# Banded attention with high and low query halves stacked in the partitions, values as the stationary operand, and results stored turned

## The chip, the cores and the metric

The kernel runs on one core of one Trainium2 chip. The metric is the device time of the core in microseconds (us), the median of three runs: 2661.86 us for the kernel before (2660.55 to 2664.36).

## The reference, cut to what matters

The whole program is a hybrid encoder block over 2048 tokens of width 1024: one projection of x, two attention mixers, a merge, a layer norm, a mixture of experts and a second layer norm. The change touches mixer A and the places where its result is read.

```python
proj = h @ w_in[l]
aq, ak, av, bq, bk, bv, gpre = jnp.split(proj, IN_SPLITS, axis=-1)
aq = apply_rope(aq ...)      # 8 heads of 64
ak = apply_rope(ak ...)      # 2 heads of 64
oa = swa_sink_attention(aq, ak, av, sinks[l])

def swa_sink_attention(q, k, v, sinks):      # chunks of 64; own chunk and the previous one
    sc = einsum('bnqkgd,bnjkd->bnkgqj', qc, kb) * (d ** -0.5)
    m = maximum(max(sc, -1), sink)
    e = exp(sc - m)
    p = e / (sum(e, -1) + exp(sink - m))
    o = einsum('bnkgqj,bnjkd->bnqkgd', p, vb)

mix = (ga * (oa @ w_proj_a[l]) + gb * (ob @ w_proj_b[l])) @ w_out[l]
```

## The kernel before, in words

Every number is float32, and products on TensorE are made from two parts of a number, a high part (the value rounded to the engine's fast format) and a low part (what is left), as high x high + low x high + high x low. ScalarE makes the high part with a copy, VectorE the low part with a subtraction. A PSUM tensor is turned (transposed) by TensorE with an identity.

The program has phases, each with its own semaphores and a barrier at its end. The phase with the prefix `j` is the projection of q, k and v with the banded attention A inside it; `b` is attention B with the gate projection; `m` the merge; then routing and the experts. Names of tensors carry the prefix: `j_qa` is `qa` of phase j.

**Projection phase (L144 to L895).** It goes over 16 tiles of 128 tokens. `over_tiles` writes tiles 0, 1, 14 and 15 out and the others as a loop of two tiles a turn. Each engine has its own program, and its order is written by hand. On TensorE a middle tile t is: `group` 0 (24 products of 512 columns: the A queries), `scores_of(t-1, g)` for the two key heads g, group 1 (24 products of 256 columns: A keys and values), `turn_p(t-1, 0)`, group 2, `turn(t, 0)`, `turn_p(t-1, 1)`, `values_of(t-1, 0)`, group 3, `turn(t, 1)`, `turn(t, 2)`, `values_of(t-1, 1)`, group 4, `turn(t, 3)`. So the attention of a tile runs inside the next tile's projection.

- `scores_of(t, g)` makes four blocks of 128 queries x 128 keys into one PSUM bank. The stationary operand is `qa[rows, half]`: 64 partitions of key head g, high or low in the free dimension. A block is three products, L427 (high q, high k), L428 (high q, low k), L429 (low q, high k).
- VectorE takes maxima (`maxima`, L742 to L747). ScalarE makes the exponentials with their sums (`exps`, L556). VectorE makes the denominators and their reciprocals (`invert`, L752, L754). TensorE turns the four blocks of exponentials (`turn_p`, L440). ScalarE and VectorE split them into `th` and `tl` (L565, L758).
- `values_of(t, g)` has the turned exponentials stationary and 128 columns of values (high and low of one head side by side) moving: L451 and L452, eight products for each g.
- `result` (L765, L767, L770, VectorE) adds the halves and multiplies by the reciprocals. `store_o` (SyncE) writes the result to `oa`, tokens x 512, in four DMAs a tile, with 256 bytes in a run.
- GpSimd has one add for each rotation (`add`, L519). `rotate` is VectorE's part of it (L794, L797, L799). `pieces` and `low` split the turned q and k into high and low (L584, L811).
- After the last tile SyncE stores its result (L274), and the phase's barrier follows. `load_chunk0` has by then loaded what attention B starts with, the four lambda vectors among it (L294).

**Merge phase (L1491 to L2007).** It also goes over 16 tiles. Tile t's 512 columns of `oa` and 512 of `ob` are loaded to `oin`. TensorE turns all 8 pieces of 128 columns (`turn`, L1671) into `pt`. ScalarE and VectorE split them (`high_ab` L1815, `low_ab` L1929), and the products with w_proj_a, w_proj_b and w_out follow. Tile t+1 is turned before the w_out product of tile t-1. GpSimd adds the gated halves (L1894).

Of the kernel before, what the change touches and what calls it, by code (L numbers as in the profile page):

```python
# [95 lines left out]
O_STORES = 16 * 4  # L96


class Chunk0:


    def __init__(self, ph, lam):
# [8 lines left out]
        self.lam = lam  # L111
# [32 lines left out]
def project_phase(nc, x_cols, w_in, positions, inv_freq, sinks, w_hi, w_lo, cos_t, sin_t, nsin_t, ident, xt_hi, xt_lo, qk_hi, qk_lo, v_hi, v_lo, oa,  # L144
# [15 lines left out]
    with Phase(nc, "j") as ph:  # L160
        x_in = chunk0.rows[:, 0, :]
        pr = chunk0.rows[:, 1, 0:BANK].rearrange("p (b n) -> p b n", b=NB)
        o = chunk0.rows[:, 1, BANK:].rearrange("p (c g j d) -> p c g j d", c=2, g=A_KV, j=2)
# [3 lines left out]
        by_sin = ph.sb("by_sin", [P, BANK])  # L167
# [6 lines left out]
        qa = ph.sb("qa", [P, 2, A_Q], F32R)  # L174

        ks = ph.sb("ks", [P, 2, 3 * CHUNK], F32R)
# [29 lines left out]
        pv, o_halved, o_added, o_scaled, o_stored = ph.sem("pv"), ph.sem("o_halved"), ph.sem("o_added"), ph.sem("o_scaled"), ph.sem("o_stored")  # L206
        block = ph.block()
        ROT = [j for j, g in enumerate(GROUPS) if g[1]]
        PG = [0, 1, 2, 0, 1]
        STAGED0 = {2: 0, 3: B_QK // P}  # L210
# [30 lines left out]

        def staged_of(half, r):
            if r == 0:
                return qa[:, half, :].rearrange("p (c i n) -> p c i n", c=2, n=CHUNK)
            if r == 1:
                return ks[:, half, 0:P]
            return (qkh, qkl)[half][:, STAGED0[r]:STAGED0[r] + GROUPS[ROT[r]][1] // P, :].rearrange("p i n -> p (i n)")

# [12 lines left out]
        def _(sp):  # L261
# [22 lines left out]
            def load_chunk0():  # L284
# [8 lines left out]
                for n, lam in enumerate(lambdas):  # L293
                    sp.dma_start(chunk0.lam[:, n, :], lam.to_broadcast([P, HD])).then_inc(chunk0.lam_in, 16)  # L294
# [43 lines left out]
            store_rows(sp, STAGED0[2], STAGED0[3], slice(SEQ - P, SEQ), last_stored)  # L338
            sp.wait_ge(v_lo_done, 2 * (NT - 1) + 4)
# [19 lines left out]
        def _(pe):  # L359
            pe.sem_inc(transposed, 2)  # L360

            def group(t, u, j):
# [4 lines left out]
                if j == 0:  # L367
# [8 lines left out]
                for k in range(KD):  # L376
# [12 lines left out]
                last.then_inc(product[j], 1)  # L389
# [17 lines left out]
            def scores_of(t, g, last_tile):  # L407
                pe.wait_ge(qk_lo_done, 4 * t + 4)
                if last_tile:
                    if g:  # L410
                        pe.wait_ge(scaled, 4 * t + 7)
                else:
                    after(pe, o_added, 2 * t + g - 1)
                rows = slice(g * HD, (g + 1) * HD)
                qh, ql = (qa[rows, half, :] for half in range(2))
                for b in range(NB):
                    out = blocks(unit_bank(g, last_tile))[:, b, :]
                    if b >= 2:
                        k_hi, k_lo = (ks[rows, half, 0:P] for half in range(2))
                    elif isinstance(t, int) and t == 0:  # L420
                        k_hi, k_lo = (ks[rows, half, 0:CHUNK] for half in range(2))
                        out = out[:, 0:CHUNK]
                    else:
                        k_hi, k_lo = (ks[rows, half, :].rearrange("p (n c) -> p n c", c=CHUNK)[:, 0:3:2, :] for half in range(2))
                        out = out.rearrange("p (n c) -> p n c", c=CHUNK)
# [17 lines left out]
            def values_of(t, g, u, last_tile):  # L443
# [3 lines left out]
                for b in range(NB):  # L447
# [2245 lines left out]
```

## Time and profile before

| | |
|---|---|
| median of the runs | 2661.86 us |
| the profiled execution's own time | 2663.14 us |
| its span, first to last instruction | 2661.4 us |
| TensorE busy (matmul / weight load) | 94% / 79% |
| VectorE, ScalarE, GpSimd busy | 62%, 46%, 17% |
| mean granted TensorE clock | 0.969 |
| DMA | 535.86 MB, 201 GB/s |

Busy shares are of the whole span; the phases have different limits, so what an edit is worth has to be read in its phase. The projection phase lies at about 15 to 548 us of the span, attention B at 550 to 1243 us, the merge at 1244 to 1676 us. PE is the TensorE matmul, PEld its weight load, DVE VectorE, ACT ScalarE, POOL GpSimd, SP SyncE. A matmul's duration in the trace is its latency; how fast matmuls follow one another is read from the distance of their starts.

### The profile page before, as it was taken

What the parts mean: (1) busy time and instruction counts of PE and PEld (TensorE: products, weight loads), DVE (VectorE), ACT (ScalarE), POOL (GpSimd) and SP (SyncE); (2) the same over time, 40 slices, a digit from 0 to 9 for tenths busy, and PEclk for the clock granted to TensorE, in tenths of its full rate; (3) what the DMA queues carried; (4) which work ended last, traced back from release to release, by engine and by line L of the source; (5) the groups of instructions that cost most, each with busy time, mean ns of one, the idle gap of its engine ahead of it and who ended that gap; (6) DMA issues with size and microseconds to landing.
All of it is one profiled execution on the core that took longest, in us unless ns stands there. A gap on an engine that the chain in (4) does not pass through costs nothing. (4 is left out here: it accounts for less than half of the span.)

```text
span 2661.4 us, 42306 instructions
## 1 busy us (share of the span) xinstructions
PE 2491.0 (94%) x12879; PEld 2092.6 (79%) x12880; DVE 1658.8 (62%) x3322; ACT 1217.2 (46%) x2075; POOL 452.3 (17%) x526
## 2 busy tenths in 40 slices
PE   5999999979999999998999999499999999999990
PEld 4888888868888888887788887388888888888880
DVE  5655455567677776766644455775785557657856
ACT  4333232244454544545111112375785557657856
POOL 0111111110110111100223331111211121112110
PEclk9999999989999999999999999599999999999995
DMA  6333333566756757535544434487897789769957
GB/s 199 122 106 102 102 102 102 153 182 194 213 182 194 216 172 205 196 132 214 177 136 139 142 111 166 171 293 278 284 382 245 226 296 327 242 225 324 381 158 260
DMA packets 233100, 535.86 MB, mean 201 GB/s; under 512 B 42945, under 2 KB 93377, under 8 KB 230961
## 3 DMA queue, kind: packets, MB, share of 16 engines
q1 hardware_dynamic: 164560, 422.55, 45.9%
q0 software_dynamic: 16416, 56.57, 8.8%
q10 hardware_dynamic: 52032, 55.61, 6.0%
q8 instruction: 48, 0.79, 0.1%
q14 instruction: 44, 0.35, 0.0%
HBM read 415.63 MB, written 119.01 MB: 201 GB/s over the span
## 5 line engine op out<-in xcount | busy, mean ns | idle before, releaser
L2543 DVE TENSOR_TENSOR e_wl<-rw_raw,e_wh 128x1024 fp32r<-128x1024 f32 (+1 forms) x384 | 446.6, 1218 | 24.7 <-ACT e_wh L2456 24.6
L2456 ACT ACTIVATE e_wh<-rw_raw 128x1024 fp32r<-128x1024 f32 (+1 forms) x384 | 376.9, 1049 | 6.5 <-PEq L74 6.5
L1228 PE MATMUL b_pg<-b_g_wh,jb_w_low 128*128 128x512 f32 x1024 | 336.6, 402 | 1.4 <-DVE b_g_out L1437 1.1
L2406 PE MATMUL e_p_gu<-e_wh,e_xh 128*128 128x512 f32 (+1 forms) x784 | 310.8, 396 | 0.8 <-DVE e_xl L2548 0.8
L2408 PE MATMUL e_p_gu<-e_wl,e_xh 128*128 128x512 f32 (+1 forms) x784 | 306.4, 391 | 0.0
L2407 PE MATMUL e_p_gu<-e_wh,e_xl 128*128 128x512 f32 (+1 forms) x784 | 305.9, 390 | 0.0
L1228 PEld LDWEIGHTS b_pg<-b_g_wh,jb_w_low 128*128 128x128 f32 x1024 | 185.1, 189 | 36.1 <-issue 3.8
L1286 ACT ACTIVATE b_th<-b_t 128x512 fp32r<-128x512 f32 (+3 forms) x160 | 85.3, 533 | 263.4 <-PE b_t L1210 255.2
L1228 PE MATMUL b_pg<-b_g_wl,jb_w_low 128*128 128x512 f32 x512 | 204.5, 400 | 0.0
L1377 DVE TENSOR_SCALAR_CACHE_REDUCE b_sc<-b_s 128x512 f32<-128x512 f32 (+4 forms) x320 | 175.8, 580 | 34.8 <-PE b_s L1199 32.7
L386 PE MATMUL j_pg<-qkv_w_hi,j_xh 128*128 128x512 f32 (+1 forms) x512 | 192.4, 376 | 2.4 <-DVE qkv_w_lo L682 2.4
L388 PE MATMUL j_pg<-qkv_w_lo,j_xh 128*128 128x512 f32 (+1 forms) x512 | 187.6, 366 | 0.0
L387 PE MATMUL j_pg<-qkv_w_hi,j_xl 128*128 128x512 f32 (+1 forms) x512 | 187.0, 365 | 0.0
L2408 PEld LDWEIGHTS e_p_gu<-e_wl,e_xh 128*128 128x128 f32 x784 | 147.6, 188 | 31.4
L2406 PEld LDWEIGHTS e_p_gu<-e_wh,e_xh 128*128 128x128 f32 x784 | 147.7, 188 | 30.9 <-issue 1.2
L2407 PEld LDWEIGHTS e_p_gu<-e_wh,e_xl 128*128 128x128 f32 x784 | 147.9, 189 | 28.3
L2418 PE MATMUL e_py<-e_wh,e_hh 128*128 128x512 f32 x392 | 161.1, 411 | 0.0
L1279 ACT ACTIVATE b_sc<-b_sc,b_nb 128x128 f32<-128x128 f32 (+15 forms) x128 | 153.1, 1196 | 17.5 <-DVE b_nb L1392 17.5
L519 POOL TENSOR_TENSOR j_by_cos<-j_by_cos,j_by_sin 128x512 f32<-128x512 f32 x64 | 82.9, 1296 | 448.4 <-DVE j_by_sin L799 448.4
L2420 PE MATMUL e_py<-e_wl,e_hh 128*128 128x512 f32 x392 | 154.2, 393 | 0.0
L1422 DVE TENSOR_TENSOR b_tl<-b_t,b_th 128x512 fp32r<-128x512 f32 (+3 forms) x160 | 97.5, 610 | 90.3 <-ACT b_th L1286 89.1
L2419 PE MATMUL e_py<-e_wh,e_hl 128*128 128x512 f32 x392 | 153.8, 392 | 0.0
(414 smaller groups left out, 5529.3 us busy)
## 6 DMA issues: line engine op xcount, KB each, us to landing
rw_raw<-w_gate_up SPq DMA_DIRECT2D x256, 512.0 KB, 6.3
rw_raw<-w_down SPq DMA_DIRECT2D x128, 512.0 KB
jb_w_low<-xt_hi SPq DMA_DIRECT2D x64, 512.0 KB, 3.8
jb_w_low<-xt_lo SPq DMA_DIRECT2D x64, 512.0 KB, 4.8
gates<-b_g_out ACTq DMA_DIRECT2D x64, 256.0 KB, 5.8
m_gt<-gates SPq DMA_DIRECT2D x16, 1024.0 KB, 8.3
jb_lead<-qk_hi SPq DMA_DIRECT2D x36, 256.0 KB, 7.1
jb_lead<-qk_lo SPq DMA_DIRECT2D x36, 256.0 KB, 7.8
```

The costliest lines, as they stand in the source:

```text
L386: nc.tensor.matmul(out, xh[:, u, at], wh, start=(k == 0), stop=False)
L387: nc.tensor.matmul(out, xl[:, u, at], wh, start=False, stop=False)
L388: last = nc.tensor.matmul(out, xh[:, u, at], wl, start=False, stop=(k == KD - 1))
L1228: last = nc.tensor.matmul(pg[:], x_side, w_side, start=(q == 0), stop=(q == PASSES - 1))
L1377: last = nc.vector.tensor_scalar(sc[u][:, m, ks.start:end], bank[n % 4][:, 0:end - ks.start], 1.0, NEG, ALU.mult, ALU.max, accum_out=mx[:, ...
L2406: nc.tensor.matmul(p_gu[p][:], xh[:, at], hi, start=(k == 0), stop=False)
L2407: nc.tensor.matmul(p_gu[p][:], xl[:, at], hi, start=False, stop=False)
L2408: last = nc.tensor.matmul(p_gu[p][:], xh[:, at], lo, start=False, stop=(k == KD - 1))
L2418: nc.tensor.matmul(py[:, js], hh[:, at], wh[:, n, js], start=(k == 0), stop=False)
L2420: last = nc.tensor.matmul(py[:, js], hh[:, at], wl[:, n, js], start=False, stop=(k == KF - 1))
L2456: nc.scalar.activation(wh[:, slot(e, s), :], raw[:, s:s + 1, :], ACT.Copy).then_inc(w_hi, 1)
L2543: nc.vector.tensor_tensor(wl[:, slot(e, s), :], raw[:, s:s + 1, :], f(wh[:, slot(e, s), :]), ALU.subtract).then_inc(w_lo, 1)
```

## The change

The score products take a stacked stationary operand. `qa` and `ks` get the key head g in the free dimension, and in the partitions the high part of q in the 64 rows of head g and the low part in the other 64; `ks` has the high part of k in both halves, and the low part of k is in a tensor `kl` of its own. A block then is two products: `qa[:, g]` (128 partitions) with `ks[:, g]`, which makes high x high and low x high at once, and `qa[rows, g]` (64 partitions) with `kl[rows]`. So splitting q and k takes one instruction for each head and half, and a copy for k.

The exponentials are multiplied by the reciprocal before they are turned (`normalise` in place of `invert`). The values are stationary and the turned exponentials move: three products of 256 columns for each of the two chunks, and the output is the result already turned, head dimension in the partitions. `result` becomes one copy of 64 partitions. `oa` is stored turned (8 heads x 64 x tokens), with two DMAs a tile and 512 bytes in a run, and the merge loads it turned: it turns only the `ob` pieces, and splits the `oa` half straight from SBUF (`high_a`, `low_a`). On TensorE `turn_p` stands now in the middle of groups 2 and 3, and `by_sin` lies in the space of `lg`, so the lambda vectors are loaded after the last rotation.

```diff
@@ projection phase
-        qa = ph.sb("qa", [P, 2, A_Q], F32R)
-        ks = ph.sb("ks", [P, 2, 3 * CHUNK], F32R)
+        qa = ph.sb("qa", [P, A_KV, A_Q], F32R)
+        ks = ph.sb("ks", [P, A_KV, 3 * CHUNK], F32R)
+        kl = ph.sb("kl", [P, 3 * CHUNK], F32R)
...
             def store_o(t, done=o_stored):
-                sp.wait_ge(o_scaled, 2 * t + 2)
-                for c in range(2):
-                    for s in range(2):
-                        sp.dma_start(oa[bass.ds(t * P + c * CHUNK, CHUNK), :].rearrange("q (b s d) -> q b s d", s=2, d=HD)[:, :, s, :],
-                                     o[s * CHUNK:(s + 1) * CHUNK, c].rearrange("p g j d -> p (g j) d")).then_inc(done, 16)
+                sp.wait_ge(o_made, 2 * t + 2)
+                for g in range(A_KV):
+                    sp.dma_start(oa[g * GH:(g + 1) * GH, :, bass.ds(t * P, P)].rearrange("h d n -> d h n"),
+                                 o[g * HD:(g + 1) * HD].rearrange("p h c n -> p h (c n)")).then_inc(done, 16)
...
-                    nc.tensor.matmul(out, qh[:, bs], k_hi, start=True, stop=False)
-                    nc.tensor.matmul(out, qh[:, bs], k_lo, start=False, stop=False)
-                    last = nc.tensor.matmul(out, ql[:, bs], k_hi, start=False, stop=True)
+                    nc.tensor.matmul(out, qa[:, g, bs], k_hi, start=True, stop=False)
+                    last = nc.tensor.matmul(out, qa[rows, g, bs], k_lo, start=False, stop=True)
...
             def turn_p(t, g, own_tile):
-                pe.wait_ge(exped, m + 1)
+                pe.wait_ge(p_scaled, m + 1)
...
-                for b in range(NB):
-                    v = (own[:, u] if b >= 2 else back[:])[:, :, g * HD:(g + 1) * HD]
-                    nc.tensor.matmul(out, th[:, bs], v, start=True, stop=False)
-                    last = nc.tensor.matmul(out, tl[:, bs], v, start=False, stop=True)
+                for c in range(2):
+                    v = own[:, u] if c else back[:]
+                    cs = slice(c * 2 * P, (c + 1) * 2 * P)
+                    nc.tensor.matmul(out, v[:, 0, :], th[:, cs], start=True, stop=False)
+                    nc.tensor.matmul(out, v[:, 0, :], tl[:, cs], start=False, stop=False)
+                    last = nc.tensor.matmul(out, v[:, 1, :], th[:, cs], start=False, stop=True)
...
-            def invert(t, g):
+            def normalise(t, g):
                 nc.vector.reciprocal(inv[:, g, :], den[:, g, :]).then_inc(summed, 1)
+                dve.wait_ge(summed, 2 * m + 2)
+                nc.vector.tensor_tensor(pr, pr, inv[:, g, :].unsqueeze(2).to_broadcast([P, NB, P]), ALU.mult).then_inc(p_scaled, 1)
...
+                    if r < 2:
+                        for g in range(A_KV):
+                            own_rows, others = rows_of(g), rows_of(1 - g)
+                            if r == 0:
+                                low_part = banded_of(r, g, others)
+                            else:
+                                nc.vector.tensor_copy(banded_of(r, g, others), f(banded_of(r, g, own_rows)))
+                                low_part = kl[own_rows, 0:P]
+                            done = nc.vector.tensor_tensor(low_part, turned_of(r, last)[own_rows], f(banded_of(r, g, own_rows)), ALU.subtract)
@@ merge phase
-                    turn(oin[:, 1 - u, :], ab_turned)
+                    turn(oin[:, 1 - u, :], ab_turned, range(KA, KD))
...
+            def high_a(t, k, u):
+                act.wait_ge(oin_in[u], 32 * (k + 1))
+                if not (isinstance(t, int) and t == 0):
+                    act.wait_ge(a_done, t)
+                nc.scalar.activation(abh[:, 0:A_Q], oin[:, u, 0:A_Q], ACT.Copy).then_inc(a_hi, 1)
...
+            def low_a(t, u):
+                dve.wait_ge(a_hi, t + 1)
+                nc.vector.tensor_tensor(abl[:, 0:A_Q], oin[:, u, 0:A_Q], f(abh[:, 0:A_Q]), ALU.subtract).then_inc(a_lo, 1)
```

What the change does to the order of two engines in the looped tile of the projection phase is shown at two places. First TensorE, at the start of `scores_of` right behind group 0; `j_pa0` is the PSUM bank of the first key head. Before:

```order
L428 MATMUL j_pa0<-j_ks,j_qa 128x128
L429 MATMUL j_pa0<-j_ks,j_qa 128x128
L427 MATMUL j_pa1<-j_ks,j_qa 128x128
L428 MATMUL j_pa1<-j_ks,j_qa 128x128
L429 MATMUL j_pa1<-j_ks,j_qa 128x128
```

These are the end of the last block of head 0 and the first block of head 1, three products a block. In the changed kernel the same place reads:

```order
L399 MATMUL j_pg0<-jb_w0,j_xl 128x512
L400 MATMUL j_pg0<-jb_w0_low,j_xh 128x512
L421 ISA
L220 ISA
L444 MATMUL j_pa0<-j_ks,j_qa 128x128
L445 MATMUL j_pa0<-j_kl,j_qa 128x128
L444 MATMUL j_pa0<-j_ks,j_qa 128x128
```

L444 has 128 partitions, L445 has 64, and they take turns through all eight blocks. Then VectorE, from the rotation of group 2 (three rows) to the split of the second head's exponentials. Before:

```order
L794 TENSOR_TENSOR j_by_cos<-j_pg,qkv_cos 128x512
L797 TENSOR_TENSOR j_by_sin<-j_pg,qkv_nsin 128x8x32
L799 TENSOR_TENSOR j_by_sin<-j_pg,qkv_sin 128x8x32
L811 TENSOR_TENSOR j_qa<-j_pt,j_qa 128x512
L752 TENSOR_TENSOR j_den<-j_sums,j_se 128x4
L753 ISA
L754 RECIPROCAL j_inv<-j_den 128x4
L758 TENSOR_TENSOR j_tl<-j_pt,j_th 128x512
```

And in the changed kernel, where L785 is the new multiplication and L844 the low part of q:

```order
L819 TENSOR_TENSOR j_by_cos<-j_pg,qkv_cos 128x512
L822 TENSOR_TENSOR lg<-j_pg,qkv_nsin 128x8x32
L824 TENSOR_TENSOR lg<-j_pg,qkv_sin 128x8x32
L781 TENSOR_TENSOR j_den<-j_sums,j_se 128x4
L782 ISA
L783 RECIPROCAL j_inv<-j_den 128x4
L784 REGISTER_ALU
L785 TENSOR_TENSOR jb_rows<-jb_rows,j_inv 128x512
L844 TENSOR_TENSOR j_qa<-j_pt,j_qa 64x512 x2
L796 COPY jb_rows<-j_pa 64x512
L789 TENSOR_TENSOR j_tl<-j_pt,j_th 128x512
```

The denominators now stand right behind the rotation, with a multiplication of 128x512 behind them on which TensorE's second `turn_p` waits.

## Rows read from the trace of the kernel before

**Rows 1.** Busy us by stretch; columns PE, PEld, DVE, ACT, POOL, clock, DMA share, GB/s.

```profile
200.00:500.00 300.00, 300.00 (x1718) 257.95 (x1717) 154.15 (x356) 93.42 (x293) 50.34 (x39) 1.00 0.33 102
1270.00:1600.00 330.00, 329.67 (x1567) 274.91 (x1566) 161.16 (x211) 37.19 (x56) 95.30 (x40) 1.00 0.41 139
```

**Rows 2.** Timeline of PE around one tile's scores; start us, duration us, then the instruction.

```profile
225.62 0.39 PE L388 MATMUL j_pg<-jb_w_low,j_xh 128*128 128x512 f32 x1
225.94 0.32 PE L427 MATMUL j_pa<-j_ks,j_qa 64*128 64x128 f32 x1
...
228.17 0.27 PE L429 MATMUL j_pa<-j_ks,j_qa 64*128 64x128 f32 x1
228.38 0.39 PE L386 MATMUL j_pg<-qkv_w_hi,j_xh 128*128 128x256 f32 x1
228.60 0.28 PE L387 MATMUL j_pg<-qkv_w_hi,j_xl 128*128 128x256 f32 x1
228.72 0.29 PE L388 MATMUL j_pg<-qkv_w_lo,j_xh 128*128 128x256 f32 x1
```

**Rows 3.** Timeline of PEld (weight loads) at the end of those scores.

```profile
228.00 0.19 PEld L428 LDWEIGHTS j_pa<-j_ks,j_qa 64*128 64x128 f32 x1
228.11 0.19 PEld L429 LDWEIGHTS j_pa<-j_ks,j_qa 64*128 64x128 f32 x1
228.37 0.19 PEld L386 LDWEIGHTS j_pg<-qkv_w_hi,j_xh 128*128 128x128 f32 x1
```

**Rows 4.** Timeline of PE: before, in and behind `values_of` for one head.

```profile
237.03 0.39 PE L388 MATMUL j_pg<-qkv_w_lo,j_xh 128*128 128x512 f32 x1
237.27 0.60 PE L404 MATMUL j_pt<-ident,j_by_cos 128*128 128x128 f32 x4
237.70 0.60 PE L440 MATMUL j_pt<-ident,jb_rows 128*128 128x128 f32 x4
238.06 0.30 PE L451 MATMUL j_pa<-j_back,j_th 128*128 128x128 f32 x1
...
238.98 0.45 PE L386 MATMUL j_pg<-qkv_w_hi,j_xh 128*128 128x512 f32 x1
```

**Rows 5.** Timeline of DVE in the same tile.

```profile
238.91 0.41 DVE L799 TENSOR_TENSOR j_by_sin<-j_pg,qkv_sin 128x256 f32<-128x256 f32 x1
239.24 0.68 DVE L811 TENSOR_TENSOR j_qa<-j_pt,j_qa 128x512 fp32r<-128x512 f32 x1
239.84 0.89 DVE L752 TENSOR_TENSOR j_den<-j_sums,j_se 128x4 f32<-128x4 f32 x1
```

**Rows 6.** Timeline of POOL in the same tile; the number before the idle time is its duration.

```profile
239.40 1.30 POOL L519 TENSOR_TENSOR j_by_cos<-j_by_cos,j_by_sin 128x512 f32<-128x512 f32 x1 [6.29 <-DVE j_by_sin L799]
```

**Rows 7.** Timeline of DVE in the merge: a multiplication of 128x512 in SBUF.

```profile
1250.43 0.69 DVE L1923 TENSOR_TENSOR jb_rows<-jb_rows,m_ri 128x512 f32<-128x512 f32 x1
```

**Rows 8.** Timelines, first tile and last tile, PE.

```profile
53.38 0.45 PE L404 MATMUL j_pt<-ident,j_by_cos 128*128 128x128 f32 x1 [8.05 <-DVE j_qa L811]
...
517.26 0.30 PE L404 MATMUL j_pt<-ident,j_by_cos 128*128 128x128 f32 x1 [1.07 <-DVE j_qa L811]
```

**Rows 9.** Timelines of the phase's end, DVE, then SP's queue.

```profile
545.00 0.42 DVE L765 COPY jb_rows<-j_pg 128x256 f32<-128x256 f32 x1 [0.32 <-PE j_pg L452]
...
545.91 0.42 DVE L770 TENSOR_TENSOR jb_rows<-jb_rows,j_inv 128x256 f32<-128x256 f32 x1
...
546.37 2.51 SPq L274 DMA_DIRECT2D oa<-jb_rows  x4
550.27 0.64 SPq L1044 DMA_DIRECT2D jb_lead<-qk_hi  x1
```

**Rows 10.** Merge: all turns of `oin`; count, least/median/greatest ns, first and last start, form.

```profile
L1671 PE MATMUL m_pt<-ident,jb_rows x128: 270/272/476, 1244.3 to 1588.3; 128*128 128x128 f32 x128
```

**Rows 11.** Merge: the longest wait of PE; us in total, times, longest.

```profile
PE m_psa L1680 <- DVE m_abl L1929: 3.2, 1, 3.2
```

**Rows 12.** Timeline of POOL in the merge's second step.

```profile
1264.41 2.36 POOL L1894 TENSOR_TENSOR m_pa<-m_pa,m_pb 128x1024 f32<-128x1024 f32 x1 [19.06 <-DVE m_pb L1981]
```

More of the change, by code:

```diff
@@ L209, in project_phase @@
         PG = [0, 1, 2, 0, 1]
+        HALVES = range(0, KD // 2), range(KD // 2, KD)
         STAGED0 = {2: 0, 3: B_QK // P}
@@ L338, in _ @@
             store_rows(sp, STAGED0[2], STAGED0[3], slice(SEQ - P, SEQ), last_stored)
+            sp.wait_ge(rotated, 4 * NT + 2)
+            for n, lam in enumerate(lambdas):
+                sp.dma_start(chunk0.lam[:, n, :], lam.to_broadcast([P, HD])).then_inc(chunk0.lam_in, 16)
             sp.wait_ge(v_lo_done, 2 * (NT - 1) + 4)
@@ L360, in _, with group @@
             pe.sem_inc(transposed, 2)
-            def group(t, u, j):
+            def group(t, u, j, ks_=range(KD)):
                 first = isinstance(t, int) and t == 0
                 c0, rot, v = GROUPS[j]
-                if j == 0:
+                if ks_[0]:
+                    pass
+                elif j == 0:
                     pe.wait_ge(scaled, 4 * t + 4)
@@ L375, in group @@
                     pe.wait_ge(v_lo_done, 2 * t + 3)
-                for k in range(KD):
+                for k in ks_:
                     if first and k % QK == 0:
@@ L388, in group @@
                     last = nc.tensor.matmul(out, xh[:, u, at], wl, start=False, stop=(k == KD - 1))
-                last.then_inc(product[j], 1)
+                if ks_[-1] == KD - 1:
+                    last.then_inc(product[j], 1)
             def turn(t, r, last_tile):
@@ L488, in tile @@
                     turn(t, 0, last)
+                    group(t, u, 2, HALVES[0])
+                    turn(t, 1, last)
                     turn_p(t - 1, 0, False)
[L490 to L491 removed]
+                    group(t, u, 2, HALVES[1])
                     scores_of(t, 0, True)
+                    values_of(t - 1, 0, 1 - u, False)
+                    group(t, u, 3, HALVES[0])
                     turn_p(t - 1, 1, False)
[L494 to L496 removed]
+                    group(t, u, 3, HALVES[1])
                     scores_of(t, 1, True)
                     turn(t, 2, last)
+                    values_of(t - 1, 1, 1 - u, False)
                     turn_p(t, 0, True)
@@ L850, in tile @@
                         over_tables(1, 9, 13)
-                    result(t - 1, 0, False)
                     if second:
@@ L1668, in _, with turn @@
         def _(pe):
-            def turn(src, done, ks=range(KD)):
+            def turn(src, done, ks):
                 for k in ks:
@@ L1739, in step @@
                 first = isinstance(t, int) and t == 0
-                if first:
-                    pe.wait_ge(first_lo, 1)
-                elif is_tile(t):
-                    pe.wait_ge(ab_lo, t + 1)
+                if is_tile(t):
+                    pe.wait_ge(a_lo, t + 1)
+                    if not first:
+                        pe.wait_ge(ab_lo, t + 1)
                 second = isinstance(t, int) and t == 1
@@ L1747, in step @@
                     pe.wait_ge(mixed, t)
-                    turn(pa, m_turned)
+                    turn(pa, m_turned, range(KD))
                 if is_tile(t):
@@ L1762, in step @@
                         pe.wait_ge(mixed, t)
-                        turn(pa, m_turned)
+                        turn(pa, m_turned, range(KD))
                     if is_tile(t - 1):
@@ L1785, in step @@
                     product(psw, mh, ml, range(KD), KA + KB, w_done, isinstance(t, int) and t == 1)
-            pe.wait_ge(oin_in[0], 32)
-            turn(oin[:, 0, :], first_turned, range(0, KA))
             over_steps(pe, step)
```

141 lines of the change are left out of this document (72 added, 69 removed).

## The prediction

> **What bounds the kernel now.** I read the stretches first (busy time by window), because both phases that the change touches have to be judged by their own limit. From 200 to 500 us, looped tiles of the projection phase, TensorE is busy 300.00 of 300.00 us at full clock, VectorE 154, ScalarE 93, GpSimd 50; from 1270 to 1600 us, the merge, TensorE is busy 329.67 of 330 us [rows 1]. The list of waits has nothing for TensorE in the looped tiles. So in both stretches the time is the sum of TensorE's slots, and everything else counts only if it makes TensorE wait. A slot is not the duration in a row (that is latency) but the distance of two starts. Then I read the timeline of matmuls and of weight loads in one tile, VectorE and GpSimd beside them, and last the two ends of the phase, where TensorE does wait.
>
> **Scores: fewer products, but each in another array mode than the one before.** In the steady stream of 64-row products one weight load follows another after 0.11 us (228.00, 228.11) [rows 3]. The 24 products of a tile with their surroundings go from 225.62 (last product of group 0) to 228.60 (second product of group 1), 2.98 us; less a slot of 0.23 for 512 columns and one of 0.12 for 256 (228.60 to 228.72) they cost 2.63 us [rows 2]. In these are two changes of the number of rows, marked 128*128 and 64*128. At the second, the next weight load comes 0.26 us after the last one, not 0.11 (228.11, 228.37) [rows 3]: it is not loaded beside the running product, but behind it. At the first, 0.32 us lie between starts where a 512-column product takes 0.23 [rows 2]. It is the same in all 14 middle tiles.
>
> The changed kernel has 16 products in place of 24, but a 128-row and a 64-row product alternate, as the order shows. The first follows group 0 in its own mode; behind each of the 16 the mode changes, the last time into group 1. At 0.26 us each that is 4.16 us a tile, against 2.63: **+1.53 us a tile, +24.5 us over 16 tiles.** The trace has no alternation, so this is bounded: from above by 0.26; the start-to-start distance of the matmuls themselves at a change is 0.21 (228.17 to 228.38) [rows 2], and if that were all, 16 x 0.21 = 3.36 us, +0.73 a tile, +11.7. If a change cost nothing once it happens on every product, 16 x 0.11 = 1.76 us, -0.87 a tile, -13.9. I take 0.26, because it is the distance of two loads, and every load stands behind a change here.
>
> The Trainium skill has rules for both ends. "TensorEngine Tiling (Array Packing)", Key Properties, says that going to another tiling mode empties the engine; by that rule, the sum is the forecast's, and the rows agree at the two changes a tile that they have. "TensorE: Matmul & The Clock Gate", LDWEIGHTS, prices a weight load by its columns and says that the number of rows doesn't matter; by that alone 64 and 128 rows could be mixed freely, and the sum would be that of the first rival.
>
> **Values.** Before, eight products take 0.92 us for a head (238.06 to 238.98) [rows 4], 1.84 a tile. Now there are twelve of 256 columns at 0.12 [rows 2]: 1.44. -0.40 a tile, -6.4 us. No mode changes here.
>
> **The new wait: `turn_p` for the second head behind the multiplication.** Group 2 ends at 237.03 + 0.23 = 237.26. TensorE then has `turn(t, 0)` (0.43, four turns, 237.27 to 237.70 [rows 4], so 0.109 each), the values (0.72) and half of group 3 (12 x 0.227 = 2.72), and would turn the exponentials at 241.13. On VectorE the rotation's last operation starts at 238.91 and lets the next start at 239.24 [rows 5]; now the denominators stand there, the reciprocal, and a multiplication of 128x512, 0.69 us [rows 7]. But GpSimd's add for this rotation runs from 239.40 to 240.70 [rows 6], and beside it a VectorE operation on SBUF alone doesn't get through: the 128x4 addition of the denominators took 0.89 us and ended at 240.73 [rows 5], while the subtraction before it, which reads PSUM, took its usual 0.68. So the multiplication starts to work at 240.70 and ends at 241.39: TensorE waits about 0.3 us a tile, 14 tiles, **+4 us**. From 0 (if it gets in before GpSimd) to 0.6 a tile (if the denominators are held too), 8 us. Behind the waiting `turn_p` stand the rest of group 3 and all that follows; the low part of p then is ready at about 243.7, and `turn(t, 2)`, which waits for it, comes at 244.3, so it costs once.
> The skill's page "SBUF — State Buffer", in SBUF: two separate sides, calls the pair of ports that VectorE and GpSimd share an exclusive lock, taken also by a VectorE operation with two SBUF inputs against a GpSimd operation that reads SBUF. By it the loser waits for the whole add, as the 0.89 us show; if ports were shared by bandwidth, the term would be near 0.
>
> The first head's multiplication stands behind the maxima, with 1.5 groups of products (some 5.6 us) as cover, and its denominators are ready some 1.5 us after the exponentials: hidden. The other edits of the tile are VectorE and ScalarE time beside a full TensorE: two subtractions of q for one (+0.68), two copies and one more subtraction for k (about +0.7), two multiplications (+1.4), one copy in place of three operations of 0.42 in `result` (-0.6 for each head). VectorE goes from 154/300 to about 57%; nothing there is late by the rows, and if one were, the price is again a wait at a turn. `store_o` has two DMAs for four, off the path within the loop.
>
> **Ends of the projection phase.** In the first tile TensorE waits 8.05 us for the low part of q, and one more copy (0.6) and one more subtraction (0.68 [rows 5]) stand in that chain: +1.3. In the last tile a wait of 1.07 us for the same [rows 8] goes, as half of group 2 now stands before `turn(t, 1)`: -1.1. At the end, the last result took VectorE from 545.00 to 546.33 and SyncE four issues in 2.51 us, and the next phase begins 1.4 us later [rows 9]. One copy of 0.7 in place of the three (-0.6) and two issues (-1.25): -1.9. The four lambda loads move past SyncE's last stores of q and k; SyncE has the gap between those and the last values' store for it, and the lambdas are used only some 6 us into the next phase: 0, and up to +2 if the last values' store is pushed past the barrier.
>
> **Merge.** 128 turns of `oin` become 64 [rows 10]. For tiles 2 to 15 that is 14 x 4 x 0.109 = -6.1 us of TensorE's stream. For tile 0 the start hangs on ScalarE, no gain. For tile 1 TensorE already waits 3.2 us for the low part [rows 11], so its turns don't count, and the low part of the `oa` half now is a subtraction in SBUF, just when GpSimd adds for 2.36 us from 1264.41 [rows 12]: it is held to 1266.77, then 0.7, then the `ob` half 0.6: 1268.0, against 1266.4 before: +1.6. In later tiles the same hold lies under the w_out product, 48 slots of 0.227, 10.9 us. Runs of 512 bytes in place of 2 KB in the loads of `oa`: a load has a whole step for itself (96 slots and 16 turns, 23.5 us); 0.
>
> **The sum**, on the profiled execution's own 2663.14 us (2661.4 of span and 1.7 around it; 1.3 above the median): +24.5 - 6.4 + 4 + 1.3 - 1.1 - 1.9 - 6.1 + 1.6 = +15.9, 2679.0; against the median, 2677.8. I say 2677.5.
>
> **Rivals.**
> First, changes of mode cost nothing when they come on every product: the next weights are loaded beside the running product after all. -13.9 in place of +24.5: 2677.8 - 38.4 = 2639. For it: fewer products, no more columns, and the trace never shows two changes in a row. Against it: all 14 middle tiles show the 0.26 and the 0.32. It wins from a price per product below about 0.20 us: at 0.20 the 16 cost 3.20, +9.1 over the tiles, which the gains elsewhere just cancel. That is the case on the other side, 16%.
> Second, only the starts' distance of 0.21 counts: 2677.8 - 12.8 = 2665. 12%, about a third of it inside the bound of no change, the rest slower.
> Third, VectorE's extra work is later than I have it (the multiplication behind the denominators that are held as well, the k copies under GpSimd's last add, and then `turn(t, 3)`): 0.9 us a tile in place of 0.3, 14 tiles, +8.4: 2686. For it: three operations on SBUF alone are new in each tile, and GpSimd's add of 1.30 us lies right over one. Against it: VectorE is busy only 154 of 300 us [rows 1]. 8%.
> That the change doesn't do what it says is no case: the order shows 16 and 12 products where there were 24 and 16.
>
> **Numbers.** Forecast 64%, first rival 16%, second 12%, third 8%. The likeliest case alone spans 2670 to 2685. To leave out no more than two in ten, the range takes the second and most of the third and leaves out the first: 2655 to 2686. About 0.2% (5.3 us) is what a measurement can tell from no change: faster 18% (the first rival and a little beside), within it 12%, slower 70%.
>
> **What the profile after would show.** The scores of a middle tile last 4.2 us from group 0 to group 1, weight loads 0.26 apart and none pulled ahead; 3.4 or 1.8 us would be the rivals. The values last 0.72 for a head. A wait of about 0.3 us at the second `turn_p` of each tile, released by the multiplication, which is drawn out to 1.5 us or more. 1.9 us less between the last values and the next phase. Merge steps shorter by 0.44 us. I am wrong if the looped tiles get shorter.

## The result and the profile after

The changed kernel takes **2703.51 us** (median of 4 runs, 2701.86 to 2704.45) against 2662.43 us for the kernel before in the same session (2660.55 to 2664.36): ratio 1.0156, 95% interval 1.0143 to 1.0169. Slower, as forecast, but by 41 us and not by 16: 2703.5 lies outside the range of 2655 to 2686.

Where the 40.5 us between the two spans (2661.4 and 2701.9) are, by first and last start of TensorE in each phase: the projection phase, which went from 19.5 to 544.5 us, now goes from 19.3 to 588.6, **+44.2**; the gap behind it -0.9; attention B +0.8; the merge with the gap before it -4.4; the rest, experts above all, +0.8. So the merge did what was forecast, and the projection phase lost twice as much as it should have.

The stretches of the kernel after, us busy and count for PE, PEld, DVE, ACT, POOL, then the granted clock, the DMA share and GB/s. The first row answers to [rows 1]; the next three are each one looped tile, from its first score product to that of the next; the last three cut the tile that begins at 275.05.

```profile
200.00:500.00 300.00, 300.00 (x1471) 250.55 (x1470) 163.15 (x338) 93.05 (x292) 44.45 (x35) 0.94 0.31 101
242.22:275.05 32.83, 32.83 (x170) 27.17 (x169) 19.16 (x39) 11.50 (x34) 5.22 (x4) 1.00 0.32 103
275.05:310.80 35.75, 35.75 (x171) 29.88 (x169) 19.16 (x39) 10.21 (x33) 5.22 (x4) 0.90 0.29 96
379.45:413.77 34.32, 34.32 (x171) 28.66 (x169) 19.16 (x39) 11.50 (x34) 5.21 (x4) 0.95 0.30 99
275.05:278.15 3.10, 3.10 (x14) 2.17 (x12) 2.37 (x5) 0.00 (x0) 1.17 (x1) 1.00 0.79 270
278.15:284.98 6.83, 6.83 (x29) 6.36 (x30) 2.24 (x8) 1.60 (x9) 0.10 (x1) 0.50 0.00 0
284.98:290.00 5.02, 5.02 (x26) 4.11 (x25) 1.44 (x5) 1.98 (x9) 0.46 (x1) 1.00 0.00 0
```

TensorE still never waits (300.00 of 300.00), but the clock column reads 0.94 where it read 1.00. The tile that keeps its full clock takes 32.83 us; all tiles of before took 31.53. The others take 34.32 or 35.75: in them the granted clock is at its half level (1.2 of 2.4 GHz) once, for 3.4 or 6.8 us. It falls 3.1 to 4.9 us after the first score product, that is towards the end of the 16 or up to 0.9 us behind them (at 278.15, with the scores from 275.05 to 279.52), and it is mostly the dense products of group 1 that then run at half speed. So a fall of 3.4 us costs 34.32 - 32.83 = 1.49 us, one of 6.8 costs 2.92. Of the 13 tiles from 105 to 551 us two have no fall, nine the short one, two the long one: 446.13 us in all, 19.2 more than 13 full-clock tiles. The instructions are the same in all 13, so they alone don't decide where in a tile the clock falls, or whether it does.

The scores, timeline of PE, answering to [rows 2]: group 0 ends, then products of 128 and 64 rows in turn.

```profile
241.99 0.39 PE L400 MATMUL j_pg<-jb_w_low,j_xh 128*128 128x512 f32 x1
242.22 0.22 PE L444 MATMUL j_pa<-j_ks,j_qa 128*128 128x128 f32 x1
242.37 0.33 PE L445 MATMUL j_pa<-j_kl,j_qa 64*128 64x128 f32 x1
242.62 0.33 PE L444 MATMUL j_pa<-j_ks,j_qa 128*128 128x128 f32 x1
242.88 0.32 PE L445 MATMUL j_pa<-j_kl,j_qa 64*128 64x128 f32 x1
```

The starts are 0.25 to 0.26 us apart, the price that [rows 3] gave for one change of mode; 16 take 3.98 us where the 24 took 2.44.

The second `turn_p` and what it waits for, answering to [rows 4 to 6]: the timelines of DVE, of POOL and of PE.

```profile
257.09 0.15 DVE L781 TENSOR_TENSOR j_den<-j_sums,j_se 128x4 f32<-128x4 f32 x1
257.27 0.18 DVE L783 RECIPROCAL j_inv<-j_den 128x4 f32<-128x4 f32 x1
257.48 1.60 DVE L785 TENSOR_TENSOR jb_rows<-jb_rows,j_inv 128x512 f32<-128x512 f32 x1
```

```profile
257.25 1.29 POOL L541 TENSOR_TENSOR j_by_cos<-j_by_cos,lg 128x512 f32<-128x512 f32 x1 [6.32 <-DVE lg L824]
```

```profile
258.54 0.39 PE L399 MATMUL j_pg<-qkv_w_hi,j_xl 128*128 128x512 f32 x1
258.77 0.39 PE L400 MATMUL j_pg<-qkv_w_lo,j_xh 128*128 128x512 f32 x1
259.14 0.66 PE L456 MATMUL j_pt<-ident,jb_rows 128*128 128x128 f32 x4
```

The multiplication is drawn out to 1.60 us beside GpSimd's add, as forecast. It ends at 259.08, and TensorE turns 0.06 us later, at 259.14. The product before starts at 258.77, and its slot is 0.23 us (258.54 to 258.77), so TensorE could have turned at 259.00: it waits 0.14 us. Because the duration of a product reaches beyond its slot, the wait doesn't show as idle time of PE. In the list of waits it stands with the weight loads:

```profile
PEld j_pt L456 <- DVE jb_rows L785: 6.8, 14, 1.6
```

In each of the 13 tiles the `turn_p` starts 0.06 us behind the multiplication, and the slot in front of it is 0.36 to 0.40 us. The sum of the denominators (257.09) got in before the add (257.25), and the reciprocal took its 0.18 us beside it, where before the sum was held (0.89). TensorE came when I had it (3.89 us behind the end of group 2, forecast 3.87), and the add ended when I had it; but the multiplication ended 0.54 us behind the add (258.54) and not 0.69.

The waits of TensorE in the phase (us in total, times, longest), answering to [rows 8]:

```profile
PE j_pt L417 <- DVE j_qa L844: 9.1, 1, 9.1
...
PE j_pt L456 <- DVE jb_rows L785: 1.4, 2, 1.2
PE j_pt L417 <- DVE j_kl L844: 1.3, 1, 1.3
```

The first is the one of 8.05 us. The one of 1.2 (in the second line) is new and stands in tile 1 alone, where VectorE also makes the later tiles' sine tables.

The end of the phase in the timeline of SP's queue, answering to [rows 9]:

```profile
589.63 1.26 SPq L282 DMA_DIRECT2D oa<-jb_rows  x2
...
593.41 0.62 SPq L1081 DMA_DIRECT2D jb_lead<-qk_hi  x1
```

The merge's turns of `oin` (count, least/median/greatest ns, first and last start), answering to [rows 10]:

```profile
L1711 PE MATMUL m_pt<-ident,jb_rows x64: 270/273/330, 1297.3 to 1627.9; 128*128 128x128 f32 x64
```

The merge's second step, DVE and then POOL, answering to [rows 12]:

```profile
1309.04 2.57 DVE L1970 TENSOR_TENSOR m_abl<-jb_rows,jb_lead 128x512 fp32r<-128x512 f32 x1 [0.41 <-ACT jb_lead L1854]
1311.53 0.68 DVE L1974 TENSOR_TENSOR m_abl<-m_pt,jb_lead 128x512 fp32r<-128x512 f32 x1
```

```profile
1308.71 2.35 POOL L1936 TENSOR_TENSOR m_pa<-m_pa,m_pb 128x1024 f32<-128x1024 f32 x1 [19.39 <-DVE m_pb L2026]
```

64 turns for 128, and in the second step the low part, 2.57 us for 0.69, is held by the add until 1311.06, then takes the rest of its time: both as forecast. A later step takes 23.13 us for 23.58, and the one with the held low part is 1.5 us longer (20.37 for 18.85; forecast +1.6).

### The profile page after: what moved, and what is told of

The parts are those of the page before. It is cut to its first block and busy times, and to the rows that moved or that the text cites. A ratio compares the mean times of both kernels' runs of the same rounds, so it can differ in the third digit from the quotient of the medians.

```text
span 2701.9 us, 41856 instructions
## 1 busy us (share of the span) xinstructions
PE 2526.7 (94%) x12623; PEld 2109.1 (78%) x12624; DVE 1709.7 (63%) x3369; ACT 1236.4 (46%) x2137; POOL 457.4 (17%) x526
## 5 line engine op out<-in xcount | busy, mean ns | idle before, releaser
L398 PE MATMUL j_pg<-qkv_w_hi,j_xh 128*128 128x512 f32 (+1 forms) x512 | 203.2, 397 | 1.8 <-DVE qkv_w_lo L711 1.8
L399 PE MATMUL j_pg<-qkv_w_hi,j_xl 128*128 128x512 f32 (+1 forms) x512 | 197.1, 385 | 0.0
L400 PE MATMUL j_pg<-qkv_w_lo,j_xh 128*128 128x512 f32 (+1 forms) x512 | 196.7, 384 | 0.0
L2453 PEld LDWEIGHTS e_p_gu<-e_wl,e_xh 128*128 128x128 f32 x784 | 147.9, 189 | 31.6
L541 POOL TENSOR_TENSOR j_by_cos<-j_by_cos,lg 128x512 f32<-128x512 f32 x64 | 82.5, 1289 | 492.8 <-DVE lg L824 492.8
```

The source lines that it names most:

```text
L398: nc.tensor.matmul(out, xh[:, u, at], wh, start=(k == 0), stop=False)
L399: nc.tensor.matmul(out, xl[:, u, at], wh, start=False, stop=False)
L400: last = nc.tensor.matmul(out, xh[:, u, at], wl, start=False, stop=(k == KD - 1))
L2453: last = nc.tensor.matmul(p_gu[p][:], xh[:, at], lo, start=False, stop=(k == KD - 1))
```

## The experiments

A product's mode is here the number of rows, 64 or 128, that it uses. Theory A was: the alternation of modes costs its slots, and it also brings the clock down. Its rivals: the fall has another cause (B), or the slot isn't a matter of modes (C). In the cuts of code "..." stands for lines left out.

**e1: the same 16 products, four changes of mode.** The heads write different banks, so they can be interleaved; every second block begins with the low keys.

```diff
-                    scores_of(t - 1, 0, False)
-                    scores_of(t - 1, 1, False)
+                for b in range(NB):
+                    for n in range(4):
+                        g, low = n % 2, (n // 2 + b) % 2
...
+                        q, k = (qa[rows, g, bs], k_lo) if low else (qa[:, g, bs], k_hi)
+                        last = nc.tensor.matmul(out, q, k, start=n < 2, stop=n >= 2)
```

> The changed kernel with its 16 score products of a looped tile in another order: the two heads, which write different banks, side by side, and every second block with the low keys' products first, so that the row mode changes 4 times a tile and not 16 times. The products are the same. Theory A (the forecast's missing term: the alternation of 128-row and 64-row products costs its slots, and it also makes the granted clock fall to half for 3.4 us or more in nearly every tile, some 1.5 us a tile): scores 12 x 0.11 + 4 x 0.26 = 2.4 us in place of 4.0, that is -24 us over 15 tiles, and no half clock between 60 and 580 us, some -22 us more: about 2657 us. Theory B (the half clock has nothing to do with the alternation, it comes from the waits or from VectorE's new work): only -24, about 2679 us, half clock as before. Theory C (a change of mode costs nothing like 0.26, the slot grew for another reason, such as 64 rows read from the wide layout): no change, 2703 us.

Measured: 2650.43 us, ratio 0.9956 (0.9940 to 0.9973); full clock from 60 to 538 us, tiles of 30.70. A, and 7 us better than A. PE shows why:

```profile
255.62 0.33 PE L468 MATMUL j_pa<-j_ks,j_qa 128*128 128x128 f32 x2
255.88 0.44 PE L468 MATMUL j_pa<-j_kl,j_qa 64*128 64x128 f32 x4
256.25 0.66 PE L468 MATMUL j_pa<-j_ks,j_qa 128*128 128x128 f32 x4
256.84 0.44 PE L468 MATMUL j_pa<-j_kl,j_qa 64*128 64x128 f32 x4
```

Four products of 128 rows take 0.59 us to the next change, four of 64 rows 0.37. The 64 rows of one head lie in partitions 0 to 63, those of the other in 64 to 127: two such products run side by side (tested in f3 and f5). That tiles of one mode work in parallel stands in the Trainium skill, "TensorEngine Tiling (Array Packing)", Key Properties; the trace agrees, 0.37 against 0.59.

**e2: all 16 products with 128 rows.** The low keys get 128 rows for each head, the other head's are zero (cleared once by GpSimd).

```diff
-        kl = ph.sb("kl", [P, 3 * CHUNK], F32R)
+        kl = ph.sb("kl", [P, A_KV, 3 * CHUNK], F32R)
...
-                    last = nc.tensor.matmul(out, qa[rows, g, bs], k_lo, start=False, stop=True)
+                    last = nc.tensor.matmul(out, qa[:, g, bs], k_lo, start=False, stop=True)
```

> The changed kernel with the low keys in a tile of 128 rows for each head, the other head's rows zero, so that all 16 score products of a tile have 128 rows and the mode never changes. Theory A: 16 x 0.11 = 1.8 us a tile in place of 4.0 (-2.2 x 16 = -35), no half clock (-22): about 2646 us. Theory B: -35 alone, half clock stays: about 2668 us. Theory C (the slot isn't a matter of modes): 2703 us.

Measured: 2646.07 us, ratio 0.9941 (0.9925 to 0.9958). Scores 1.73 us a tile (products 0.11 apart), tile 30.59, full clock. As theory A has it; B and C fall, and the price of a change is (32.83 - 30.59) / 16 = 0.14 us on top of 0.11.

**e3: the scores' part undone**, with its layout, copies and subtractions; all else as changed.

```diff
...
-                    nc.tensor.matmul(out, qa[:, g, bs], k_hi, start=True, stop=False)
-                    last = nc.tensor.matmul(out, qa[rows, g, bs], k_lo, start=False, stop=True)
+                    nc.tensor.matmul(out, qh[:, bs], k_hi, start=True, stop=False)
+                    nc.tensor.matmul(out, qh[:, bs], k_lo, start=False, stop=False)
+                    last = nc.tensor.matmul(out, ql[:, bs], k_hi, start=False, stop=True)
```

> The changed kernel with one part undone: the scores as they were (three products of 64 rows a block, q and k in high and low halves of the free dimension, one copy and one subtraction for each). Values, the multiplication of p, the order of half groups and the merge stay changed. Theory A: the slots go back to 2.44 us a tile (-1.54 x 16 = -25) and the clock stays full (-22): about 2657 us, some 6 us under the kernel before. Theory B: half clock stays: about 2679 us. A third (the +44 us of the phase come largely from VectorE's new multiplication and the waits behind it): over 2690 us.

Measured: 2656.22 us, ratio 0.9979 (0.9969 to 0.9988), looped tiles of 31.39 at full clock. So the rest of the change is a small gain (0.14 us a tile, 1.1 in the last tile, 2.0 at the phase's end, the merge), and all of the loss lies in the scores: 47 us, of which 1.44 us a tile are slots.

One fall is left, in tile 1, and it is of use below. There the scores are those of tile 0, the first with only half of the keys: 12 of the 24 products of 64 rows have 64 moving columns in place of 128. They go from 66.06 to 68.50 us, and 0.8 us behind them the clock is at half:

```profile
66.06:69.31 3.25, 3.25 (x31) 3.18 (x31) 2.81 (x8) 1.61 (x3) 1.27 (x1) 1.00 0.93 309
69.31:72.72 3.41, 3.41 (x18) 3.41 (x17) 3.14 (x10) 1.28 (x9) 0.00 (x0) 0.50 0.01 2
```

The kernel before has the same 24 products there, and no fall.

**e4: the alternation in two stretches** with 12 dense products between them.

```diff
                     group(t, u, 0)
                     scores_of(t - 1, 0, False)
+                    group(t, u, 1, HALVES[0])
                     scores_of(t - 1, 1, False)
-                    group(t, u, 1)
+                    group(t, u, 1, HALVES[1])
```

> The changed kernel with the first half of group 1 (12 dense products, 2.7 us) put between the two heads' scores. As many products, as many changes of mode (16 a tile), but the alternation comes in two stretches of 2.0 us. Theory A1 (the clock falls because of one long alternation of 4.0 us): no half clock, about 2703 - 22 = 2681 us. Theory A2 (each short alternation is enough, or its share in the tile counts): half clock as before, about 2703 us. Theory B (no link with the alternation): 2703 us.

Measured: 2680.79 us, ratio 1.0073 (1.0056 to 1.0090). The looped tiles are 32.84 us and the clock is 1.00:

```profile
200.00:500.00 300.00, 300.00 (x1547) 248.16 (x1545) 175.11 (x357) 98.26 (x308) 48.45 (x37) 1.00 0.33 105
```

A1: nothing is taken away, the slots stay, and 22.7 us come back. This is the price of the clock, measured by itself. (The 12 products have 256 columns and take 1.54 us, not the 2.7 of the expectation.)

**f6: only 3 dense products between.**

Against e4:

```diff
-                    group(t, u, 1, HALVES[0])
+                    group(t, u, 1, range(0, 1))
                     scores_of(t - 1, 1, False)
-                    group(t, u, 1, HALVES[1])
+                    group(t, u, 1, range(1, KD))
```

> The changed kernel with only 3 dense products (0.4 us at 256 columns) of group 1 between the two heads' scores, where the earlier split had 12. If such a short break is enough: full clock, about 2681 us. If the two alternations count as one: half clock in nearly every tile, about 2703 us.

Measured: 2705.08 us, ratio 1.0166 (1.0145 to 1.0186), clock 0.95 from 200 to 500 us. 0.46 us of dense work doesn't help, 1.54 us does.

**f2: the new scores alone, in the kernel before.** The diff is that of e3 read backwards, on the other kernel; it also has `by_sin` in the space of `lg` and the lambda loads behind the last rotation, as the changed kernel has.

> The kernel before with the scores' part of the change alone (the layout of q and k, 16 products in two modes, and the copies and subtractions that belong to it); values, results and merge as before. If the slots and the clock together come from the alternation: 2662.4 + 1.54 x 16 (25) + 22 = about 2709 us, half clock in nearly every tile, and steady tiles without it of 31.53 + 1.54 = 33.07 us. If the clock needs the new order of values and turns beside it: 2687 us.

Measured: 2713.92 us, ratio 1.0203 (1.0186 to 1.0220), clock 0.94 from 200 to 500 us, tiles of 34.4 to 34.5 with the short fall and 35.9 with the long one. The fall needs nothing of the rest of the change but that move. It is 5 us above the expectation; 3 of them are that here not one tile keeps its full clock, where the changed kernel has two.

**f1: no alternation at all, but a long run.** The kernel before, each block's three 64-row products issued twice.

```diff
+                    for _ in range(2):
                         nc.tensor.matmul(out, qh[:, bs], k_hi, start=True, stop=False)
                         nc.tensor.matmul(out, qh[:, bs], k_lo, start=False, stop=False)
                         last = nc.tensor.matmul(out, ql[:, bs], k_hi, start=False, stop=True)
```

> The kernel before with the three 64-row products of every score block issued twice (48 a tile in place of 24): a run of short products in one mode, about 5.1 us long, longer than the alternation of 4.0 us. If the clock falls because TensorE computes with short or half-high products for so long: half clock in most tiles, 2662 + 24 x 0.11 x 16 (42) + 22 = about 2726 us. If it falls because of the alternation, in which every weight load stands behind a product: full clock, 2662 + 42 = 2704 us.

Measured: 2746.36 us, ratio 1.0321 (1.0300 to 1.0342). My theory was too narrow: the clock falls in every tile of the loop without a change of mode inside the run. It is 20 us more than I expected for this case, mostly because 12 of the 15 falls are the long one. The windows of one tile, from its first score product, and of the stretch:

```profile
200.00:500.00 300.00, 300.00 (x1664) 264.07 (x1663) 127.00 (x300) 79.07 (x247) 41.89 (x32) 0.91 0.29 91
...
289.46:293.46 4.00, 4.00 (x40) 4.00 (x40) 2.35 (x6) 0.14 (x1) 1.27 (x1) 1.00 0.60 201
293.46:300.29 6.83, 6.83 (x33) 6.71 (x33) 1.04 (x4) 1.46 (x9) 0.00 (x0) 0.50 0.00 0
```

After 4.0 us of 64-row products 0.11 us apart (3.4 to 5.0 in the 15 tiles), the half level for 6.8 us. In these rows the engine was never idle.

**g1: as long a run of short products, but of 128 rows.** The kernel of e2 with each block's two products issued three times.

```diff
+                    for _ in range(3):
                         nc.tensor.matmul(out, qa[:, g, bs], k_hi, start=True, stop=False)
                         last = nc.tensor.matmul(out, qa[:, g, bs], k_lo, start=False, stop=True)
```

> The kernel whose 16 score products a tile all have 128 rows (2646 us), with each block's two products issued three times: 48 short products of full height, about 5.3 us, as long as the run of 48 products of 64 rows of which a clock at half speed and 2746 us came. If a long run of short products (128 columns) is enough for the clock to fall, whatever their height: half clock for 6.8 us in most tiles, 2646 + 32 x 0.11 x 16 (56) + some 42 = about 2744 us. If it takes half-high products (64 rows), full clock and 2702 us.

Measured: 2703.60 us, ratio 1.0154 (1.0125 to 1.0183).

```profile
200.00:500.00 300.00, 300.00 (x1771) 261.02 (x1770) 163.40 (x340) 94.24 (x295) 45.77 (x35) 1.00 0.32 102
279.19:284.50 5.31, 5.31 (x50) 5.31 (x48) 2.37 (x6) 1.56 (x9) 1.28 (x1) 1.00 0.47 157
```

48 products in 5.31 us, as many and as fast as in f1, with the same 128 columns, and the clock stays at 1.00 in all looped tiles. The two runs don't stand on the same kernel (f1 on the one before, g1 on the changed one), but groups 0 and 1 around the scores are the same; of the run itself only the rows differ. So the number of products and of loads alone doesn't bring the clock down. In front of the falls in the loop stood half-high products, alone (f1) or in turn with full ones and with gaps (the changed kernel).

But the height isn't all. In tile 1 of g1, where 24 of the 48 products have 64 moving columns, the clock does fall, with 128 rows throughout:

```profile
71.24 0.28 PE L446 MATMUL j_pa<-j_kl,j_qa 128*128 128x64 f32 x1
71.35 0.28 PE L445 MATMUL j_pa<-j_ks,j_qa 128*128 128x64 f32 x1
```

```profile
68.53:72.60 4.07, 4.07 (x38) 4.07 (x37) 2.43 (x7) 1.34 (x2) 1.28 (x1) 1.00 0.77 255
72.60:79.43 6.83, 6.83 (x34) 6.83 (x34) 3.42 (x11) 1.54 (x9) 0.00 (x0) 0.50 0.01 2
```

They start 0.11 us apart as well: half the columns in the same time. So in front of the falls in these runs stood products with fewer rows, products with fewer columns, or gaps at each change of mode, and no wait of TensorE. Which share each has, no run tells apart.

**f3 and f5: the two heads in turn.** The three 64-row products of before, for head 0 and head 1 alternately; f3 in the changed kernel, f5 in the kernel before, where nothing else is touched.

```diff
+                for b in range(NB):
...
+                    for q, k in ((0, 0), (0, 1), (1, 0)):
+                        for g in range(A_KV):
...
+                            last = nc.tensor.matmul(out, qa[rows, q, bs], keys, start=(q + k == 0), stop=(q == 1))
```

> The changed kernel with the three 64-row products a block of before, but the products of the two heads in turn: one head's operands lie in partitions 0 to 63, the other's in 64 to 127, and they write different banks. In the paired order of the changed kernel's scores, four 64-row products of two heads took 0.37 us with a change of mode in it, where four of 128 rows took 0.59. If such a pair runs side by side: 12 x 0.11 less a tile, 15 tiles, -20 us from the 2656 us of the same kernel with the heads one behind the other: 2636 us. If not (each product takes its 0.11): 2656 us.

> The kernel before, with nothing but the order of its 24 score products changed: the two heads in turn. Side by side: 2662.4 - 20 = 2642 us; otherwise 2662 us.

Measured: f3 2641.44 us, ratio 0.9923 (0.9908 to 0.9938); f5 2652.99 us, ratio 0.9969 (0.9958 to 0.9980). In both, 24 products take 1.49 us (2.44 before), 0.95 less and not 1.32: 24 x 0.062. In f3, timeline of PE:

```profile
251.12 1.56 PE L457 MATMUL j_pa<-j_ks,j_qa 64*128 64x128 f32 x24
252.61 0.38 PE L394 MATMUL j_pg<-qkv_w_hi,j_xh 128*128 128x256 f32 x1
```

In f3 the tile is 30.45, against e3 the 0.95 less in full. In f5 it is 30.7 to 31.6, because the first `turn_p` now comes before the exponentials are done:

```profile
PE j_pt L460 <- ACT j_se L577: 4.1, 12, 0.8
```

The changed kernel's place for `turn_p`, half a group later, is what gives these back in f3.

**f4: f3, and the sine tables earlier**, six of their steps at the end of the first tile, where VectorE is idle.

```diff
                     low(3)
+                    over_tables(1, 0, 6)
...
-                    if second:
-                        over_tables(1, 0, 3)
                     normalise(t - 1, 0)
...
                     if second:
-                        over_tables(1, 3, 9)
+                        over_tables(1, 6, 9)
```

> The changed kernel with paired heads in its scores, and six of the 17 steps that make the later tiles' sine tables moved from the second tile to the end of the first, where VectorE is idle. In the second tile of the changed kernel TensorE waits 1.2 us for p's multiplication and 1.4 us in front of or in group 4, behind those steps; if they are what holds it, -2.6 us more: 2634 us. If the steps now hold the second tile's first rotation: 2636 us or more.

Measured: **2638.82 us, ratio 0.9916 (0.9903 to 0.9930)**, the best version: 23 us faster than the kernel before, 65 faster than the changed one. The second tile goes from 31.65 us in f3 to 30.47, so the waits in it came from those steps; the rest of its -2.6 lies in the first tile (1.2 us earlier at the first score) and is no clean gain of the edit.

## Why the prediction was right or wrong

The step that failed is in the first paragraph: "So in both stretches the time is the sum of TensorE's slots". I read the clock of 1.00 in [rows 1] as a property of the stretch, not of what is done in it, and priced the new slots alone. In the changed kernel the slots of group 1 themselves got longer, behind the scores, with the clock at half: 23.6 us that the sum put at nothing. No rival had a term for it, and so the range ended at 2686. By terms, in us:

| Term | forecast | measured, and from what |
|---|---|---|
| Scores' slots | +24.5 | +22.5: 1.44 x 14 tiles (32.83 - 31.39) and 2.3 in the last (e4 - e3) |
| Granted clock | none | +23.6: 19.2 in 13 tiles, 2.9 in tile 1, 1.5 in the last (against e4) |
| Values | -6.4 | -3.9: 0.26 a tile (1.59 for 1.85) x 14, and 0.3 in the other slots of the tiles |
| Wait at the second `turn_p` | +4 | +2.0: 0.14 x 14. With the values it makes the 0.14 a tile by which e3 is shorter (31.39 for 31.53) |
| Tile 1 | none | +2.5: the waits behind the table steps (35.26 in e4, for 32.84) |
| First tile | +1.3 | -1.5: its wait grew by 1.1, nearly as forecast, but TensorE came to it 1.05 earlier, so it ends at 53.4 as before; behind it the clock is at half until 56.28 and not until 59.35 |
| Last tile's wait | -1.1 | -1.1 (33.70 in e3, 34.80 before) |
| Phase's end | -1.9 | -0.9, and -2.0 in e3 |
| Merge | -4.5 | -4.4 |
| Attention B, experts | 0 | +1.6, spread over both and not explained |
| Sum | +15.9 | +40.4 (spans: +40.5) |

Without the clock the measured terms come to +16.8, beside a forecast of +15.9. That is in part luck: the values gave 2.5 less and tile 1 took 2.5 more than I had, the slots, the wait and the first tile 2.0, 2.0 and 2.8 less.

- **Slots: right.** The choice of 0.26 for each of the 16 changes was the likeliest case, and the traces bear it out (3.98 us for 16 products; forecast 4.16 with the edge). The first rival (changes free) is refuted by the changed kernel itself, the second (0.21) too. One point of the first did come true in another form: 64-row products of two heads do overlap, if nothing changes the mode between them and they use different rows and banks.
- **The wait behind the multiplication: mechanism right, size off.** The multiplication was held until GpSimd's add ended, 1.60 us for 0.69, and the second `turn_p` was released by it in each tile. But it ended 0.54 us behind the add and not 0.69, and so TensorE waited 0.14 us and not 0.3. A term that is the difference of two near times doubles or halves by 0.15 us in one of them. The third rival (VectorE later) is refuted for the loop, and true for tile 1, which I hadn't looked at apart: there VectorE has 17 more table operations.
- **Merge, last tile: right**, by their own steps.
- **Phase's end.** The copy and the two issues are as forecast, and e3 has the 2.0; in the changed kernel 2.5 us lie between SyncE's last issue and the next phase where e3 and before have 1.4. So has e4, whose phase ends with the same instructions as the changed kernel's; e1 has 1.7. So those instructions alone don't make the 1.1, and what does stays open.

Could the profile of before have told it? Not the price, and hardly the mechanism: all of its falls stand in or right behind a wait of TensorE, as at 49.11 us in the wait of 8.05. But a clock of 0.969 over the span said that it can fall, and the change made the thinnest stretch of the tile longer by 1.5 us. That was reason for a rival with a slower kernel and a range that reaches further up. The Trainium skill ("TensorE: Matmul & The Clock Gate", HAM oscillation) speaks of idle gaps before the clock falls; by that rule a stream without gaps between its instructions keeps its clock. In the looped tiles of g1 it does; in f1, with 300.00 of 300.00 us busy and a clock of 0.91, it doesn't.

What stays open besides: which share the gaps and which the half-high products have in the changed kernel's fall (no run has such gaps between 128-row products alone), and what decides, among tiles of the same instructions, when the clock falls and for how long.

## What to carry to other kernels

Count changes of TensorE's row mode as a cost of their own (here 0.14 us each on top of the product's 0.11), and put products of one mode together; fewer products can be slower. Where only half of the rows are needed, give the other half to an independent product in another bank (24 in 1.49 us for 2.44); that was worth 9 us with no other edit (f5), 15 where nothing waits behind it (f3 against e3). A long stretch of thin work on TensorE can have a second price, paid behind it: read the clock column there in the new kernel, and if it has fallen, break the stretch up with dense products (1.54 us of them were enough here, 0.46 were not).

## What the runs showed of the hardware

- The granted clock fell to its half level although TensorE had work without a break: 3.1 to 4.9 us after the first of 16 products of 128 and 64 rows in turn, and 3.4 to 5.0 us after the first of 48 products of 64 rows 0.11 us apart. In the looped tiles it didn't after 5.31 us of 128-row products 0.11 us apart, nor with 24 products of 64 rows in 2.44 us, nor with two alternations of 1.9 us and 1.54 us of dense products between. Where part of the products had 64 moving columns (tile 1), it fell with 128 rows too (g1), and once behind 2.44 us of 64 rows (e3).
- A fall in such a stream lasted 3.41 or 6.83 us and cost the tile 1.49 or 2.92 us.
- A change between 128 and 64 rows cost 0.14 us beside the 0.11 of the product.
- Two 64-row products with operands in different halves of the partitions and outputs in different banks start 0.06 us apart on average, where one head's alone start 0.11 apart.
